# Input projection of block 1 as three rounded products, and the normalise-and-split stages of block 2 shared out over three engines

## The chip, the cores and the metric

One core of a Trainium2 chip runs the whole program in one launch. The time is device microseconds of that core. Five engines run side by side and meet only at semaphores: TensorE (PE in the profile, its weight loads PEld), VectorE (DVE), ScalarE (ACT), GpSimd (POOL) and SyncE (SP, which only issues transfers).
## The reference

Two transformer blocks in float32 on 512 latent tokens and 256 context tokens, 1024 wide. Each begins every sub-layer with a root-mean-square norm and a modulation by a shift and a scale that come from a small matrix product of the condition vector (six of them for each layer). Block 1 has a mixer (attention and gated linear attention) and a mixture of experts; block 2 has two layers of a mixer and a squared-ReLU network.

```python
def modulate(h, shift, scale):
    return h * (1 + scale) + shift
...
    dq_l, dk_l, dv_l, gq_l, gk_l, gv_l, gr_l, lrf_l, lrb_l = split_in_proj(h_lat @ w_in)
    dq_c, dk_c, dv_c, gq_c, gk_c, gv_c, gr_c, lrf_c, lrb_c = split_in_proj(h_ctx @ w_in)
...
def log_gate(lowrank, w2, b):
    return jax.nn.log_sigmoid((lowrank @ w2 + b).astype(jnp.float32)) / GLA_GATE_TAU
```

`w_in` of block 1 is 1024 x 3104: six blocks of 512 columns, and 32 columns at the end, the gate rank (`lrf`, `lrb`, 16 each), which `log_gate` multiplies by a 16 x 256 matrix for each direction.

```python
    for i in range(DEPTH_2):
        ...
        h = modulate_2(rms_norm_2(x, g_norm1[i]), sh1, sc1)
        hc = modulate_2(rms_norm_2(ctx, g_norm1[i]), mc[0], mc[1])
        p = h @ w_in[i]
        ...
        x_new = x_new + gt2 * squared_relu_mlp(modulate_2(rms_norm_2(x_new, g_norm2[i]), sh2, sc2),
                                               ffn_w1[i], ffn_w2[i])
```

## The kernel before

The program is a row of stages. `fence` ends a stage: TensorE, ScalarE, VectorE and GpSimd each drain and wait until all four are there (SyncE only reads the count). Inside a stage each engine runs its own hand-written list; no scheduler reorders it. Tokens lie in six tiles of 128 (`ALLT`: four latent, `LAT`, and two context). PSUM has eight banks of 512 floats.

Four kinds of stage matter here.

- **Normalise, block 1** (`pe_norm`, `act_norm`, `dve_norm`). The scaled tiles `XE` are transposed on TensorE, and ScalarE (first half of the 1024 rows) and VectorE (second half) apply scale and shift while they copy PSUM into `hT`.
- **Input projection, block 1** (`pe_lin`, `each_lin`, `sp_lin` with `BL1`). 32 groups of 8 products of 128 x 128 by 128 x 512, float32, six banks. After each group `pe_mod` does one of 32 modulation steps: 8 products with two columns of condition vectors, four of them side by side on the array, against 2 MB of weights that GpSimd loads into one of two slots (`load_mod`, which waits until the step before the last has run). After every fourth step VectorE copies the sum out (`dve_mod`) and ScalarE writes it to memory and waits for it to land (`act_mod`). Last come six groups of 32 columns for the gate rank.
- **Gates, block 1** (`pe_gates`, `act_gates`, `dve_gates`). The gate rank is transposed tile by tile, copied, multiplied by `w2a`, copied, and goes through Abs, Exp and Ln, each over 3072 columns.
- **Normalise and split, block 2** (`pe_norm_split`, `act_norm_split`, `dve_norm_split`), twice in each of two layers: m = 0 ahead of the input projection, m = 1 ahead of the network (six tiles, but four in m = 1 of the second layer). ScalarE spills x to memory, takes six sums of squares, and for each of the twelve half tiles applies scale and shift into a buffer `NTMP` (four instructions), then rounds it to float32r (`hh`, one instruction). VectorE scales the tiles (`XM`) and subtracts the rounded from the exact one to get the rest (`hl` or `hm`, one instruction for each half tile). For m = 0 the rest lies on top of x, so it waits until the spill has landed. GpSimd meanwhile runs `pool_params2`: it loads seven small parameters, and builds in memory a table `rpbd` of 3840 KB from the position bias, whose landing it waits for before it reaches the fence.

Behind m = 0 comes the projection of block 2 (`pe_proj`), which already is made of three rounded products (`three`: high by high, high by low, low by high). ScalarE rounds each weight piece (`proj_round`), GpSimd makes its rest (`pool_proj`), and GpSimd first issues four loads of the table (`load_table`).

## Time and profile before

| | before |
|---|---|
| median of 3 runs | 4182.31 us (4179.34 to 4189.25) |
| the profiled execution, its time | 4173.02 us |
| its span, first to last instruction | 4171.2 us |
| TensorE busy | 3509.4 us, 84% of the span |
| VectorE, ScalarE, GpSimd busy | 1398.7, 1081.0, 532.9 us |
| mean granted clock of TensorE | 0.916 of 2.4 GHz |

The shares of busy time are means over some forty stages. Since every stage ends in a fence, a stage's length is that of its slowest engine, and what is saved in one stage is saved in the total, unless a transfer that crosses the fence takes it back. A busy microsecond saved on an engine that isn't the last in its stage is worth nothing.

### The profile page before, as it was taken

Reading aid. Unit: us, or ns where it says so; the run is one execution under the profiler, and the core shown is the slowest. Engines: PE = TensorE matmul, PEld = TensorE weight load, DVE = VectorE, ACT = ScalarE, POOL = GpSimd, SP = SyncE. Lnnn points to the kernel's source line nnn. Section 1 sums busy time; section 2 is a strip of 40 time slices with the busy share of each in tenths; the row PEclk is TensorE's granted clock in tenths of the full one; section 3 lists DMA queues with packets and bytes.
Section 4 is the critical chain, followed back from the end, with each engine's and each line's share of the span. In section 5 each row is a group of like instructions: output and inputs, shape, how many; then the busy total and the mean of one; then the engine's idle time right before and its main releaser. Section 6 shows DMA issues by size and latency. Waiting matters only on the chain. (4 is left out here: it accounts for less than half of the span.)

```text
span 4171.2 us, 40026 instructions
## 1 busy us (share of the span) xinstructions
PE 3509.4 (84%) x15659; PEld 2278.5 (55%) x15659; DVE 1398.7 (34%) x2471; ACT 1081.0 (26%) x1967; POOL 532.9 (13%) x427
## 2 busy tenths in 40 slices
PE   5997666587881998788999699999498898997998
PEld 2334554222230784445665388888386455656886
DVE  1104642100003355562112233333364561123444
ACT  2001421111113225443111322121324542104221
POOL 0000000100001425122110000000145222200000
PEclk9997877799995999899999899999799999998999
DMA  7773013699995311002112221221521002223222
GB/s 286 273 274 143 1 44 110 254 428 428 428 428 170 100 37 32 8 1 91 61 61 81 71 71 61 64 68 51 168 77 33 8 34 90 89 81 131 91 91 81
DMA packets 143624, 531.84 MB, mean 128 GB/s; under 512 B 8802, under 2 KB 47128, under 8 KB 120416
## 3 DMA queue, kind: packets, MB, share of 16 engines
q1 hardware_dynamic: 117184, 388.89, 24.8%
q0 software_dynamic: 19792, 102.32, 7.5%
q10 hardware_dynamic: 6480, 38.34, 2.4%
q8 instruction: 112, 1.84, 0.2%
q14 instruction: 56, 0.46, 0.0%
HBM read 486.74 MB, written 42.78 MB: 127 GB/s over the span
## 5 line engine op out<-in xcount | busy, mean ns | idle before, releaser
L507 PE MATMUL ps<-ring,hT 128*128 128x512 f32 (+1 forms) x1056 | 440.1, 576 | 11.8 <-DMA ring<-in_w_out_dram 9.1
L507 PEld LDWEIGHTS ps<-ring,hT 128*128 128x128 f32 x1056 | 196.0, 197 | 255.3 <-issue 252.1
L2556 PE MATMUL ps<-hT_hi,w_hi 128*128 128x512 f32 (+1 forms) x768 | 276.2, 360 | 20.5 <-DVE w_lo L2610 20.5
L1671 PE MATMUL ps<-wp_hi,hT_hi 128*128 128x512 f32 (+2 forms) x608 | 221.8, 365 | 65.6 <-POOL wp_lo L1650 65.6
L2556 PE MATMUL ps<-hT_lo,w_hi 128*128 128x512 f32 (+1 forms) x768 | 276.9, 361 | 0.0
L2556 PE MATMUL ps<-hT_hi,w_lo 128*128 128x512 f32 (+1 forms) x768 | 276.3, 360 | 0.0
L2562 PE MATMUL ps<-w_hi,h_hi 128*128 128x512 f32 x640 | 253.7, 396 | 0.0
L2562 PE MATMUL ps<-w_hi,h_lo 128*128 128x512 f32 x640 | 253.7, 396 | 0.0
L2562 PE MATMUL ps<-w_lo,h_hi 128*128 128x512 f32 x640 | 253.7, 396 | 0.0
L1671 PE MATMUL ps<-wm_hi,hT_hi 128*128 128x512 f32 x480 | 215.6, 449 | 28.4 <-POOL wm_lo L2326 28.4
L1884 PE MATMUL ps<-Z 64*128 64x256 f32 (+3 forms) x576 | 201.7, 547 | 28.3 <-DVE small L2026 12.0
L1673 PE MATMUL ps<-wp_hi,hm_lo 128*128 128x512 f32 (+2 forms) x608 | 220.0, 362 | 0.0
L1672 PE MATMUL ps<-wp_lo,hT_hi 128*128 128x512 f32 (+2 forms) x608 | 219.4, 361 | 0.0
L2356 PE MATMUL ps<-ring,pj 128*128 128x512 f32 x480 | 215.6, 592 | 0.0
L2579 ACT ACTIVATE w_hi<-ring 128x2048 fp32r<-128x2048 f32 x64 | 121.9, 1908 | 328.4 <-PE ps L2562 326.8
L1673 PE MATMUL ps<-wm_hi,hm_lo 128*128 128x512 f32 x480 | 191.8, 400 | 0.0
L1672 PE MATMUL ps<-wm_lo,hT_hi 128*128 128x512 f32 x480 | 191.6, 399 | 0.0
L1443 PE MATMUL ps<-ring,Z 128*64 128x512 f32 x512 | 142.7, 721 | 54.1 <-ACT Z L1465 54.1
L2610 DVE TENSOR_TENSOR w_lo<-ring,w_hi 128x2048 fp32r<-128x2048 f32 x64 | 146.5, 2292 | 80.3 <-ACT w_hi L2579 80.3
L2556 PEld LDWEIGHTS ps<-hT_hi,w_hi 128*128 128x128 f32 x768 | 145.3, 189 | 45.6 <-issue 21.3
L1671 PEld LDWEIGHTS ps<-wp_hi,hT_hi 128*128 128x128 f32 x608 | 115.4, 190 | 84.7 <-issue 66.0
L2632 DVE TENSOR_TENSOR pj<-pj,ps 128x512 f32<-128x512 f32 x140 | 95.5, 686 | 195.0 <-PE ps L2562 195.0
(415 smaller groups left out, 5651.8 us busy)
## 6 DMA issues: line engine op xcount, KB each, us to landing
pj<-in_expert_w_up_dram SPq DMA_DIRECT2D x32, 2048.0 KB, 18.3
pj<-in_expert_w_down_dram SPq DMA_DIRECT2D x32, 2048.0 KB, 19.7
ring<-in_expert_w_gate_dram SPq DMA_DIRECT2D x32, 2048.0 KB, 16.1
ring<-in_ffn_w_dram SPq DMA_DIRECT2D x64, 1024.0 KB, 5.3
Z<-in_w_mod_dram POOLq DMA_DIRECT2D x24, 2048.0 KB, 8.0
ring<-in_w_in_dram SPq DMA_DIRECT2D x46, 1024.0 KB, 5.9
Z<-in_w_ada_dram POOLq DMA_DIRECT2D x8, 2048.0 KB, 8.1
ring<-in_w_in_dram SPq DMA_DIRECT2D x6, 2048.0 KB, 13.0
```

Source lines behind the costliest of these rows:

```text
L507: last = nc.tensor.matmul(bank(i % nb, w), lhs(k, t), s[:, k * w:k * w + w], start=(k == 0), stop=(k == nk - 1))
L1443: last = nc.tensor.matmul(bank(2 + m)[64 * x:64 * x + 64, :], xgT[:, k, 64 * x:64 * x + 64], mslot[2 * m + x][:, 512 * k:512 * k + 512], s ...
L1671: nc.tensor.matmul(out_, a_hi, b_hi, start=first, stop=False)
L1672: nc.tensor.matmul(out_, a_hi, b_lo, start=False, stop=False)
L1673: return nc.tensor.matmul(out_, a_lo, b_hi, start=False, stop=final)
L1884: return nc.tensor.matmul(A.lat(u, x) if k0 == 0 else A.ctx(u, x), S["kq"](p, x, "q")[rs, P * t:P * t + P], S["kq"](p, x, "k")[rs, P * k0: ...
L2356: last = nc.tensor.matmul(bank(6 + u % 2), YB(j % 3, k, t), w[:, 512 * k:512 * k + 512], start=(k == 0), stop=(k == 3))
L2556: last = nc.tensor.matmul(bank(i % 8, c1 - c0), W[a][:, k, :], r[:, k, c0:c1], start=(k == 0 and r is hhk and a == 0), stop=(k == KT - 1 a ...
L2562: last = nc.tensor.matmul(bank(i % 8), H1[hb % 2][a][:, k, P * what:P * what + P], W[b][:, k, :], start=(k == 0 and a == b), stop=(k == 3 ...
L2579: act.activation(WHI[x % 2], raw[x % 4], ACT.Copy).then_inc(w_hi_ok, 1)
L2610: nc.vector.tensor_tensor(WLO[x % 2], raw[x % 4], WHI[x % 2], ALU.subtract).then_inc(w_lo_ok, 1)
L2632: nc.vector.tensor_tensor(y, y, bank(i % 8), ALU.add).then_inc(out_read, 1)
```

## The change

1. Block 1's normalise stage also rounds: ScalarE and VectorE write the modulated half tile to a buffer (`N1T`, in `pj`), then a rounded copy to `hhk`; the twelve rests go to GpSimd (eight, `pool_norm1`) and VectorE (four, `rest1`). They lie on top of x in `xl`, so x is loaded again later (`x_again`).
2. The projection takes the weights in twelve pieces of four row blocks by 512 columns (1 MB) in three slots. ScalarE rounds a piece, VectorE writes its rest over the raw piece, and TensorE does three products for each one before. A group's first four row blocks run in one piece and its last four in the next, so every tile is visited twice; a modulation step follows every second visit, 32 steps as before.
3. The gate rank is computed transposed: weights of 32 columns against 512 and 256 tokens. The gates stage has no transposes; its six products have 33 rows (both directions and a row of ones), Abs reads PSUM, and Exp, Ln and the last VectorE step work in two halves.
4. Block 2's normalise-and-split: ScalarE and VectorE share the sums of squares (half the tiles each) and the half tiles (first half, second half); GpSimd scales every second tile, and makes two of three rests. `NTMP` has a slot for each half tile.
5. `pool_params2` keeps a memset; its transfers are issued by SyncE (`sp_params2`), ahead of the third weight piece. `load_table` moves behind the second piece on GpSimd. The second context is loaded six stages earlier.

```diff
-                    if nb == 6 and i <= 3 * MSTEPS - EARLY:
-                        pe_mod(pe, EARLY + i - 1)
...
-        BL1 = [(0, 512, LAT), (512, 1024, ALLT), (1024, 1536, ALLT), (1536, 2048, ALLT), (2048, 2560, ALLT),
-               (2560, 3072, LAT), (3072, 3104, ALLT)]
+        BL1 = [(0, 512, LAT), (512, 1024, ALLT), (1024, 1536, ALLT), (1536, 2048, ALLT), (2048, 2560, ALLT), (2560, 3072, LAT)]
...
+        def used1(p, x):
+
+            j = x // 2
+            return (w1_half, j + 1) if x % 2 == 0 else (mm_done, p.done(G1[j] + len(BL1[j][2]) - 1))
...
+            for x in range(N1 + 1):
+                if x >= 3:
+                    sp.wait_ge(*used1(p, x - 3))
...
+        def act_split1(act, p, x):
+
+            if x > N1:
+                return
+            act.wait_ge(w1_in[x % 3], 16 * (x // 3 + 1))
+            if x >= 2:
+                act.wait_ge(*used1(p, x - 2))
+            for raw_, hi, _ in w1_parts(x):
+                last = act.activation(hi, raw_, ACT.Copy)
...
+            dve.wait_ge(w1_hi_ok, x + 1)
+            for raw_, hi, lo in w1_parts(x):
+                last = nc.vector.tensor_tensor(lo, raw_, hi, ALU.subtract)
+            last.then_inc(w1_lo_ok, 1)
...
+            for x in range(N1):
+                j, half = x // 2, x % 2
+                pe.wait_ge(w1_lo_ok, x + 1)
+                for m, t in enumerate(BL1[j][2]):
+                    i = G1[j] + m
+                    if half == 0 and i >= 6:
+                        pe.wait_ge(EV[p.own[i - 6]], p.val[i - 6])
+                    for k in range(4 * half, 4 * half + 4):
+                        o = 2048 * (x % 3) + 512 * (k % 4)
+                        last = three(bank(i % 6), hhk[:, k, P * t:P * t + P], hmk[:, k, P * t:P * t + P],
+                                     w1_hi_k(x, k % 4), w1_lo[:, o:o + 512], k == 0, k == KT - 1)
+                    if half:
+                        last.then_inc(mm_done, 1)
+                    elif t == BL1[j][2][-1]:
+                        last.then_inc(w1_half, 1)
+                    q += 1
+                    if q % 2 == 0:
+                        pe_mod(pe, EARLY + q // 2 - 1)
+            pe.wait_ge(w1_lo_ok, N1 + 1)
+            for g, (c0, c1) in enumerate(((0, 512), (512, 768))):
+                i = 32 + g
+                pe.wait_ge(EV[p.own[i - 6]], p.val[i - 6])
+                for k in range(KT):
+                    last = three(bank(i % 6, c1 - c0)[0:32, :], w1_hi[:, 32 * k:32 * k + 32], w1_lo[:, 32 * k:32 * k + 32],
+                                 hhk[:, k, c0:c1], hmk[:, k, c0:c1], k == 0, k == KT - 1)
+                last.then_inc(mm_done, 1)
+
+        def act_lin1(act, n, p):
+            q = 0
...
+                    if half and p.own[i] == "a":
+                        act.wait_ge(mm_done, p.done(i))
+                        act_put(*BL1[j][:2], t, bank(i % 6)).then_inc(evac_a, 1)
+                    q += 1
+                    if q % 8 == 0:
+                        act_mod(act, q // 8)
+                act_split1(act, p, x + 2)
+            act.wait_ge(mm_done, p.done(32))
...
+        def pool_norm1(pool):
+            for i in range(2 * TA):
+                if i % 3 != 2:
+                    rest1(pool, i)
...
+            for t in range(TA):
+                nc.tensor.matmul(bank(t), lrt[t // 4][:, P * (t % 4):P * (t % 4) + P], w2a[0:33, :], start=True, stop=True).then_inc(mm_done, 1)
...
+                act.activation(sp_[:, t, :], bank(t), ACT.Abs)
             act.drain()
-            act.activation(sp_, zc, ACT.Abs)
+            for b in range(2):
...
         def pool_params2(pool, l):
+            pool.memset(rpt, 0.0).then_inc(rp_ok, 1)
+
+        def sp_params2(sp, l):
...
-            pool.wait_ge(rp_in, 32 * l + 16)
-            pool.dma_start(rpbd.ap()[l].rearrange("r (m n) -> r m n", n=P), rpt[0:120, :].unsqueeze(1).broadcast_to([120, 64, P])).then_inc(rp_in, 16)
-            pool.wait_ge(rp_in, 32 * l + 32)
...
+            sp.wait_ge(rp_in, 32 * l + 16)
+            sp.wait_ge(x_out, 16 * (2 * l + 1))
+            sp.dma_start(rpbd.ap()[l].rearrange("r (m n) -> r m n", n=P), rpt[0:120, :].unsqueeze(1).broadcast_to([120, 64, P])).then_inc(rp_in, 16)
...
                 c0, c1 = BL2[l][j][:2]
+                if x == 2:
+                    sp.wait_ge(stage_done, f0)
+                    sp_params2(sp, l)
...
-            load_table(pool, l, 0)
             for x in range(len(R.pieces)):
+                if x == 2:
+                    pool.wait_ge(rp_in, 32 * l + 32)
+                    load_table(pool, l, 0)
...
-                if i >= 3:
-                    act.wait_ge(hl_ok, p.g0 + i - 2)
+            for t in range(nt):
+                act.wait_ge(mm_done, p.done(2 * t))
...
+                act.activation(hhk[:, 0:4, 128 * t:128 * t + 128], NTMP(2 * t).rearrange("p (k n) -> p k n", k=4), ACT.Copy).then_inc(hh_ok, 1)
...
+        def norm_rest(eng, m, g0, i):
+
+            t, h = i // 2, i % 2
+            lo = (hmk, hlk)[m]
+            eng.wait_ge((hh_ok, hh_v)[h], g0 + t + 1)
+            eng.tensor_tensor(lo[:, 4 * h:4 * h + 4, 128 * t:128 * t + 128], NTMP(i).rearrange("p (k n) -> p k n", k=4),
+                              hhk[:, 4 * h:4 * h + 4, 128 * t:128 * t + 128], ALU.subtract)
...
+            V.memset(st[:, 40:41], 0.0)
+            dve.drain()
+            for t in range(na, nt):
+                V.tensor_tensor_reduce(JUNK[1 + t - na], xl[:, t, :], xl[:, t, :], 1.0, st[:, 40:41], ALU.mult, ALU.add, st[:, 16 + t:17 + t])
...
+            scale(0)
+            scale(2)
+            for t in range(nt):
+                if t == 1 and nt > 4:
+                    scale(4)
+                dve.wait_ge(mm_done, p.done(2 * t + 1))
+                for k in range(4):
+                    kk = 4 + k
+                    c = 48 * (t // TL) + 24 * m + kk
+                    last = V.tensor_scalar(NTMP(2 * t + 1)[:, 128 * k:128 * k + 128], bank((2 * t + 1) % 8)[:, 128 * k:128 * k + 128],
+                                           Ac[:, l, t // TL, m, kk:kk + 1], modc[:, l, c:c + 1], ALU.mult, ALU.add)
+                last.then_inc(ht_tmp_v, 1)
+                dve.drain()
+                V.tensor_copy(hhk[:, 4:8, 128 * t:128 * t + 128], NTMP(2 * t + 1).rearrange("p (k n) -> p k n", k=4)).then_inc(hh_v, 1)
             if m == 0:
...
+            pool.wait_ge(rstd_ok, n["rstd"])
+            for t in range(1, nt, 2):
+                pool.tensor_scalar(XM(t), xl[:, t, :], st[:, 32 + t:33 + t], 1.0, ALU.mult, ALU.mult).then_inc(xn_p, 1)
+            if m == 0:
+                pool.drain()
+                pool.wait_ge(x_out, 16 * (2 * l - 1))
+                pool.wait_ge(xn_ok, TA + TL + (p.g0 + nt) // 2)
+            for i in range(2 * nt):
+                if i % 3 != 2:
+                    norm_rest(pool, m, p.g0, i)
 
...
+            sp.wait_ge(stage_done, 4 * 3)
+            sp.dma_start(xl[:, 0:TL, :], I["x"][0].rearrange("(t p) d -> p t d", p=P)).then_inc(x_again, 16)
...
+            sp.dma_start(xl[:, TL:TA, :], I["ctx_2"][0].rearrange("(t p) d -> p t d", p=P)).then_inc(x_in, 16)
```

TensorE at the start of the projection of block 1, before (`ring` holds float32 weights, `hT` the tokens; the rows with `Z` and `small` are a modulation step):

```order
L507 MATMUL ps<-ring,hT 128x512 [waits slot0_in,stage_done]
L507 MATMUL ps<-ring,hT 128x512 x7
L272 MATMUL ps<-Z,small 2x512 [waits mod_slot4_in]
L272 MATMUL ps<-Z,small 2x512 x7
L507 MATMUL ps<-ring,hT 128x512 x8
```

and of the change, from the second product of the eighth row block that it visits, across the first modulation step:

```order
L1838 MATMUL ps<-w_hi,hT_hi 128x512
L1839 MATMUL ps<-w_lo,hT_hi 128x512
L1840 MATMUL ps<-w_hi,hm_lo 128x512
L277 MATMUL ps<-Z,small 2x512 [waits mod_slot4_in]
L277 MATMUL ps<-Z,small 2x512 x7
L1838 MATMUL ps<-w_hi,hT_hi 128x512
```

Eight products between two modulation steps have become 24, and the modulation step itself is the same.

VectorE in the normalise-and-split stage m = 0 of block 2's first layer, before:

```order
L2456 TENSOR_SCALAR small<-small 128x6 [waits sumsq,x_in,stage_done]
L2459 RECIPROCAL small<-small 128x6 [waits std]
L2470 TENSOR_SCALAR pj<-xl,small 128x1024 x6
L2465 TENSOR_TENSOR hm_lo<-Z,hT_hi 128x4x128 [waits hh_ok,x_out]
L2465 TENSOR_TENSOR hm_lo<-Z,hT_hi 128x4x128 [waits hh_ok] x11
```

and of the change (`ISA` is the sum of squares of one tile, three in all; the pair L2651 and L2655 stands six times):

```order
L2629 ISA pj,small<-xl,small 128x1024
...
L2633 TENSOR_SCALAR small<-small 128x6 [waits sumsq]
L2636 RECIPROCAL small<-small 128x6 [waits std]
L2640 TENSOR_SCALAR pj<-xl,small 128x1024 x2
L2651 TENSOR_SCALAR Z<-ps,small 128x128 [waits mm_done]
L2651 TENSOR_SCALAR Z<-ps,small 128x128 x3
L2655 CAST hT_hi<-Z 128x4x128
...
L2618 TENSOR_TENSOR hm_lo<-Z,hT_hi 128x4x128 [waits hh_ok,xn_p,x_out]
L2618 TENSOR_TENSOR hm_lo<-Z,hT_hi 128x4x128 [waits hh_v]
```

VectorE has gained three sums of squares and six half tiles and has lost eight rests, and its four rests now stand behind all its half tiles.

GpSimd at the same place, before:

```order
L1562 DMA Z<-in_gm_w_s_2_dram 128x4x128
L1565 MEMSET Z 128x128
L1567 DMA Z<-in_na_rpb_2_dram 120x31 [waits rp_ok]
L1569 DMA rpbd<-Z 7680x1x128 [waits rp_in]
L1579 DMA Z<-rpbd 64x14x64 [waits rp_in,stage_done]
L1579 DMA Z<-rpbd 64x14x64 x3
```

and of the change (eight rests in six rows, then the first two weight pieces of the projection):

```order
L1719 MEMSET Z 128x128 [waits stage_done]
L2667 TENSOR_SCALAR pj<-xl,small 128x1024 [waits rstd_ok]
L2667 TENSOR_SCALAR pj<-xl,small 128x1024 x2
L2618 TENSOR_TENSOR hm_lo_55<-Z,hT_hi_49 128x4x128 [waits hh_ok,xn_ok,x_out]
L2618 TENSOR_TENSOR hm_lo_55<-Z,hT_hi_49 128x4x128 [waits hh_v] x2
...
L1817 TENSOR_TENSOR wp_lo_57<-ring,wp_hi_56 128x2048 [waits wr_ok,stage_done]
L1817 TENSOR_TENSOR wp_lo_57<-ring,wp_hi_56 128x2048 [waits wr_ok]
L1741 DMA Z<-rpbd 64x14x64 [waits rp_in]
```

The wait for `rp_in`, the table's landing, has moved from ahead of the fence to behind two weight pieces of the next stage.

## Rows read from the trace of the kernel before

**Rows 1.** Timeline, TensorE in block 1's projection: start us, us, engine line op tiles

```profile
72.50 7.13 PE L507 MATMUL ps<-ring,hT 128*128 128x512 f32 x16
...
79.56 1.90 PE L272 MATMUL ps<-Z,small 128*2 128x512 f32 x16
...
81.39 7.13 PE L507 MATMUL ps<-ring,hT 128*128 128x512 f32 x16
```

**Rows 2.** Busy time by stretch: us, PE, PEld, DVE, ACT, POOL, clock, DMA share, GB/s

```profile
100.00:150.00 50.00, 50.00 (x174) 18.87 (x173) 6.20 (x9) 1.79 (x3) 3.80 (x6) 1.00 0.75 281
```

**Rows 3.** Timeline, the six gate-rank groups

```profile
348.22 15.21 PE L507 MATMUL ps<-ring,hT 128*128 128x32 f32 x96
```

**Rows 4.** The chain that ended last, block 2's network: start us, us, what

```profile
3789.07 47.69 PE ps L2556 x192
...
3859.25 22.40 PE ps L2556 x96
```

**Rows 5.** Transfers in block 1's projection: KB each, median us to landing

```profile
Z<-in_w_mod_dram POOLq DMA_DIRECT2D x24, 2048.0 KB, 8.0
```

**Rows 6.** Timeline, block 1's normalise stage and the projection's first product

```profile
53.57 1.37 DVE L472 TENSOR_SCALAR hT<-ps,small 128x128 f32<-128x128 f32 x4 [2.17 <-PE ps L415]
...
62.21 7.13 PE L507 MATMUL ps<-ring,hT 128*128 128x512 f32 x16 [1.87 <-DVEq L214]
```

**Rows 7.** Timeline, the gates stage, up to the next stage's first product

```profile
493.26 1.34 DVE L945 MEMSET hT<- 32x1536 f32 x1 [0.46 <-POOLq L214]
...
505.38 2.76 ACT L937 ACTIVATE Z<-Z 128x3072 f32<-128x3072 f32 x1
...
516.40 3.36 DVE L949 SCALAR_TENSOR_TENSOR Z<-Z 128x3072 f32<-128x3072 f32 x1 [21.80 <-ACT Z L941]
519.84 6.22 PE L964 MATMUL ps<-Z,consts 128*128 128x256 f32 x16 [15.18 <-DVEq L214]
```

**Rows 8.** Timeline, block 2's first normalise-and-split stage and its fence

```profile
1307.93 0.39 SPq L2834 DMA_DIRECT2D xl<-in_ctx_dram  x1
...
1313.27 1.06 ACT L2427 ACTIVATE Z<-xl 128x1024 f32<-128x1024 f32 x1 [10.55 <-DMA xl<-in_ctx_dram]
...
1323.65 1.50 ACT L2441 ACTIVATE Z<-ps,small 128x128 f32<-128x128 f32 x4 [2.33 <-PE ps L2417]
...
1325.77 1.49 ACT L2441 ACTIVATE Z<-ps,small 128x128 f32<-128x128 f32 x4
...
1327.52 2.82 POOL L1569 DMA_DIRECT2D rpbd<-Z  x1 [14.21 <-DMA Z<-in_na_rpb_dram]
...
1328.13 1.29 DVE L2465 TENSOR_TENSOR hm_lo<-Z,hT_hi 128x512 fp32r<-128x512 f32 x2 [2.44 <-DMA xspill<-xl]
...
1349.04 0.69 DVE L2465 TENSOR_TENSOR hm_lo<-Z,hT_hi 128x512 fp32r<-128x512 f32 x1 [1.41 <-ACT hT_hi L2445]
...
1357.00 3.71 ACT L1638 ACTIVATE wp_hi<-ring 128x2048 fp32r<-128x2048 f32 x2 [7.99 <-POOLq L214]
...
1360.40 9.05 POOL L1650 TENSOR_TENSOR wp_lo<-ring,wp_hi 128x2048 fp32r<-128x2048 f32 x2
```

**Rows 9.** Timeline, the same fence in the second layer

```profile
3001.67 3.71 ACT L1638 ACTIVATE wp_hi<-ring 128x2048 fp32r<-128x2048 f32 x2 [7.87 <-POOLq L214]
```

**Rows 10.** Groups of instructions by shape: line engine op, xcount | busy us, mean ns

```profile
L2326 POOL TENSOR_TENSOR wm_lo<-ring,wm_hi 128x2048 fp32r<-128x2048 f32 x24 | 109.3, 4559 | 396.2 <-ACT wm_hi L2317 396.2
L2183 POOL TENSOR_TENSOR Z<-pj 128x256 f32<-128x256 f32 x24 | 14.7, 612 | 52.1 <-ACT pj L2161 51.9
...
L2380 DVE CAST hT_hi<-hT 128x3072 fp32r<-128x3072 f32 x2 | 3.5, 1760 | 17.2 <-DMA hT<-hTd 17.2
...
L2021 DVE CUSTOM_DVE_ANT_0 Z<-ps,Z,small 128x512 f32<-128x512 f32 x5 | 3.8, 751 | 0.6
```

**Rows 11.** Timeline of GpSimd and of VectorE in block 2's first projection

```profile
1402.63 4.79 POOL L1650 TENSOR_TENSOR wp_lo<-ring,wp_hi 128x2048 fp32r<-128x2048 f32 x1 [12.52 <-ACT wp_hi L1638]
...
1403.62 4.36 DVE L835 TENSOR_TENSOR Z<-pj 128x512 f32<-128x512 f32 x1
```

290 lines of the change are left out of this document (182 added, 108 removed).

## Prediction

> **What bounds the kernel now.** I read the page, then the timeline of each stage that the change touches, then groups by shape. No single engine bounds the whole: each stage lasts as long as its slowest engine and the fences add these up. So I cost the change stage by stage, from fence to fence.
>
> In block 1's projection TensorE is never idle. A group of eight float32 products starts at 72.50 and the modulation step behind it at 79.56, the next group at 81.39: 7.06 us and 1.83 us, 8.89 us a period [rows 1]. The granted clock there is 1.00 and the DMA engines are busy 0.75 of the time at 281 GB/s [rows 2]. The six gate-rank groups take 15.21 us for 96 instructions that each produce 32 columns [rows 3]. The rounded form has a price in block 2's network: 96 products of 128 x 512 in 22.40 us, 0.2333 us each, and 47.69 us for the first 192, which is 2.9 us over twice 22.40: the start, which I read as TensorE coming out of idleness on the lower of its clock's two levels [rows 4].
>
> In block 2's normalise-and-split ScalarE sets the pace: four modulations start at 1323.65, the next four at 1325.77, so 2.12 us a half tile and 25.4 us for twelve [rows 8]. VectorE ends at 1349.7, yet the next stage begins at 1357.00 with ScalarE released by GpSimd's queue after 7.99 us: GpSimd had issued the table write only at 1327.52 and waited for its landing [rows 8]. The second layer shows the same, 7.87 us [rows 9]. The first layer also waits for its context: issued at 1307.93, and ScalarE's first square runs at 1313.27 [rows 8].
>
> **The change part by part.** Durations are from the profiled execution.
>
> *Projection of block 1.* Three products for one: 24 x 0.2333 = 5.60 us for the 7.06. I add 0.20 for the passage to the modulation step (an estimate: 16 float32 instructions spaced 0.43 apart end 0.2 short of 7.06). The step stays 1.83. Period 7.63, saving 1.26, times 32: **-40.3**. The start: TensorE now idles longer ahead of the stage, +2.9 [rows 4]; in return the first modulation load (8.0 us [rows 5]) is no longer waited for; before it cost about 1.4 us (first group at 62.21 [rows 6], second at 72.50, one period is 8.89). Together **+1.5**. Gate rank: 24 products over 512 tokens and 24 over 256, 5.6 + 2.8 = 8.4 us, one copy of no more than the 0.69 us that 512 columns take VectorE [rows 8], against 15.2: **-6.2**. Rounding a piece takes 1.9 us on ScalarE (3.71 for two [rows 8]) and its rest about 2.7 on VectorE (four times the 0.69 of 512 columns [rows 8]); a piece lasts TensorE four or six visits, 15 to 23 us, so 4.6 us is hidden, unless ScalarE stands behind a modulation write. Sum -45, between -50 and -38.
>
> The row gives 0.2333 us a product. The Trainium skill, TensorE: Matmul & The Clock Gate, section Back-to-back issue gap, gives about 216 ns for 512 columns on the faster clock; by that the 768 products would be 13 us cheaper. The row is of this very form, so it decides.
>
> *Normalise of block 1.* VectorE was first released at 53.57 and takes 1.37 us for four modulations [rows 6]. Now each of its six half tiles is 1.37, a drain of 0.1 and a cast: 1.760 us for 3072 columns [rows 10] makes 0.35 for 512. That is 10.9 us; a weight rest 2.7, four rests 2.8: 16.4. Meanwhile GpSimd makes eight rests. Its price for 512 columns lies between 0.612 (256) and 4.559 (2048); on the line between them 1.18 [rows 10]. The two engines get in each other's way: a VectorE instruction with two SBUF inputs of 512 columns, 0.69 us elsewhere, took 4.36 us while GpSimd's 4.79 us subtraction ran, and ended with it [rows 11]. A wait is thus bounded by nothing and a whole GpSimd rest, 1.18. I take half, 0.6, on each of six casts, and 1 us over the rests: 21 us, so the projection starts near 75 instead of 62.2: **+12** (+8 without waits, +17 with full ones).
>
> No row shows a cast beside GpSimd. The Trainium skill, SBUF — State Buffer, section Who interferes with whom, says that casts in the two-port mode also take the pair of ports that GpSimd uses, and that the one who comes second is blocked for the whole instruction. By that rule the six waits exist; by the row alone they could be zero and this term +8.
>
> *The stage behind the projection.* Two memsets on VectorE's path (1.34 us for 1536 columns [rows 7], 768 here: 0.7), and 2 MB of x again. At 281/0.75 = 375 GB/s [rows 2] that is 5.6 us of transfer in a stage whose last work is small writes: 0 to 5.6, I take 1.3. **+2**.
>
> *Gates.* Before: 493.26 to 519.84, 26.6 us [rows 7]. After: six products with float32 instructions. TensorE comes from idleness, so near twice the 0.88 us that two instructions take in [rows 1]: 9 us for six (5.3 to 10.5). Then the last Abs 0.6, and from [rows 7] (2.76 for 3072 columns; 505.38 to 516.40 holds three passes and two table loads, so 1.3 a load) 1.3 + 2.8 + 1.3 + 2.8, half of 3.36, and 0.3: 20.1. **-6.5** (-3 to -10).
>
> *Block 2, m = 0, first layer.* The context is there: ScalarE's squares start 4.9 us earlier. Three squares instead of six, each 1.06 us and the read of its sum, about 1.2, save 3.7, but VectorE's three are longer: 0.751 us for 512 columns of an accumulating instruction [rows 10] makes about 1.4 for 1024; net -3.2. Then ScalarE does six half tiles, 12.7 us, and VectorE's six take 10.9 plus one scaling of 0.75; both end near 1328.5. The rests come last: they wait for the spill. It let VectorE go at 1328.13 [rows 8]; issued 4.6 us earlier it should land near 1324. From there GpSimd's eight, VectorE's four and some casts share the port: 9.4 + 2.8 + 1.3, end at 1337.5. The table is no longer waited for at the fence. Next stage at 1338 instead of 1357.0: **-19**. *Second layer*: no context wait to save, but its spill has the queue more to itself: **-16.5**.
>
> *m = 1.* No spill wait, no table. First layer: squares -3.2. Loop 25.4 + 0.8 before; after, VectorE: 6 x (1.82 + 0.6) + 0.75, 1.0 for its later start, rests 4.0: 20.3; together **-9**. Second layer, four tiles: squares -2, 17.8 against 9.7 + 1.0 + 2.0: **-7**. Without port waits each would be 4 to 5 better.
>
> *Start of block 2's projection.* GpSimd began its first rest at 1360.40, 3.4 us after ScalarE, which had that piece ready after 1.9: four table loads stood ahead. Without them -1.5, twice: **-3**. The table (29 us from issue to landing, 1327.52 to about 1356.6 [rows 8]) is now written by SyncE once the spill has landed, at about 1325, and needed by GpSimd behind its second piece, near 1347. It waits there until some 1355, 3 us of loads follow, and TensorE asks for the third piece only after 2 x 18 us of work, near 1378: hidden with 15 us to spare. Queued behind it on SyncE is the third raw piece, needed at about 1360; if it came late it would eat into those 15 us.
>
> **Sum:** -45 + 12 + 2 - 6.5 - 19 - 16.5 - 9 - 7 - 3 = -92. The profiled execution took 4173.0 us: 4081. The median of the runs shown is 9.3 us above it, so **4090** as a median.
>
> **The rivals.**
>
> *Port worse than half* (0.14). Each cast and each VectorE rest waits out a whole GpSimd rest: +5 in block 1, about 5 in each of four stages: 4115. For it: GpSimd's queue of rests is dense. Against: ScalarE delivers only one half tile in 2.1 us, so GpSimd works 1.6 of 2.1.
>
> *No port waits, or cheaper products* (0.13). -4 in block 1, -4 to -5 in the two m = 1 stages, some in m = 0: 4074. A product below 0.2333 us, if weight loads hide better here than in the network, would also end there: each 0.01 is 8 us over 768 products. By the figure of the Trainium skill cited above the estimate would be 4077.
>
> *Transfers bound the projection* (0.06). If each 2 MB modulation load kept the 8.89 us beat, the 40 us are lost: 4130. For it: 0.75 busy would become 0.75 x 8.89 / 7.63 = 0.87. Against: between the step that frees a slot and the one that needs it lie now 7.63 + 5.80 = 13.4 us, and a load takes 8.0 [rows 5].
>
> *The clock falls in the projection* (0.03), the case on the other side. If the dense rounded products alternating with the narrow step were granted the lower level, 1.2 GHz, a period would be 2 x 7.4 + 0.2 = 15 us, 7.4 above forecast. From 92 / 7.4 = 12.4 of 32 periods on, the kernel is slower than before; all 32 make 4325. Against: 1.00 with the same narrow step today [rows 2], and the network's products run at the fast pace [rows 4].
>
> That the change does nothing (0.02, within 0.2%) would need several of these at once.
>
> **How the numbers follow.** The forecast holds 0.62, with its own range 4078 to 4105. To leave out no more than 2 in 10, the range takes in the no-waits case and the bad-port one to about 4114: 4066 to 4114. A measurement of this kernel tells about 0.2% from no change, 8 us. Faster by more than that: all but the clock case and the last, 0.95; same 0.02; slower 0.03.
>
> **What would show it.** In the changed profile: a projection period of 7.6 us and clock 1.0; VectorE's first rests around 70 and the projection's start near 75; the projection stage's end near 331; the gates stage 20 us; the first-layer m = 0 stage 30 us long with `x_out` as the last wait ahead of the rests, no 8 us of GpSimd's queue at the fence; casts of clearly more than 0.35 us where GpSimd is busy. The prediction is wrong if TensorE waits for `w_lo` in the middle of the projection, above all where a modulation write ends a piece and the next is only four visits long, if the third weight piece of block 2 arrives late behind the table, or if the casts wait in full.

## The result and the profile after

The changed kernel takes 4064.16 us (median of four runs, 4061.06 to 4067.18), the kernel before in the same comparison 4180.83: a ratio of 0.9719, 95% interval 0.97 to 0.9738. So the change saves 117 us where I had forecast 92 us, and the time lies 1.8 us below the low end of my range (4066). The direction was right and the size too small by a fifth. The profiled execution took 4065.76 us (span 4063.9), so this time profile and median agree; of the kernel before, the profile I had summed from was 8 us quicker than its median.

In the projection of block 1 the modulation steps are now 7.49 to 7.58 us apart, 7.53 in the mean, instead of 8.89 [rows 1]. Two of them (timeline of TensorE, changed kernel):

```profile
282.81 1.90 PE L277 MATMUL ps<-Z,small 128*2 128x512 f32 x16
290.33 1.90 PE L277 MATMUL ps<-Z,small 128*2 128x512 f32 x16
```

In this stretch TensorE is busy all the time, on the upper level (2.4 GHz, granted clock 1.00), and the busy share of the DMA engines went from 0.75 to 0.88 (busy time by stretch, columns as in [rows 2]):

```profile
100.00:150.00 50.00, 50.00 (x270) 31.02 (x269) 13.45 (x16) 7.75 (x9) 4.78 (x7) 1.00 0.88 335
```

Ahead of it, the normalise stage of block 1 (timeline; its first transposition starts at 49.65 us, where it was 51.49):

```profile
53.18 0.43 DVE L701 CAST hT_hi<-pj 128x512 fp32r<-128x512 f32 x1
...
53.57 2.50 POOL L688 TENSOR_TENSOR hm_lo<-pj,hT_hi 128x512 fp32r<-128x512 f32 x2 [47.65 <-ACT hT_hi L680]
54.98 1.39 DVE L701 CAST hT_hi<-pj 128x512 fp32r<-128x512 f32 x1
...
68.66 2.48 DVE L688 TENSOR_TENSOR hm_lo<-pj,hT_hi 128x512 fp32r<-128x512 f32 x4
71.23 0.79 PE L1838 MATMUL ps<-w_hi,hT_hi 128*128 128x512 f32 x1 [13.39 <-DVEq L219]
```

One cast takes VectorE 0.43 us, the next 1.39: that one lies within GpSimd's two rests (53.57 to 56.07, 1.25 us each). The four rests at the end run at 0.62 us each; GpSimd has finished by then. Behind the projection, the stage that turns the modulations (issue of the last of three small writes, and the next stage's first product):

```profile
345.52 0.31 ACTq L331 DMA_DIRECT2D modd<-Z  x1
...
351.24 1.12 PE L779 MATMUL ps<-consts,pj 128*128 128x128 f32 x4 [25.05 <-ACTq L219]
```

The gates ([rows 7] before): TensorE starts after 12 us of idleness, and its twelve instructions are 0.85 us apart, half the pace of the 0.43 us at which such instructions run on the upper level.

```profile
457.69 10.61 PE L1089 MATMUL ps<-Z,pj 33*128 33x512 f32 x12 [12.03 <-DVEq L219]
```

And block 2's first normalise-and-split, which answers to [rows 8]: the spill is issued and the squares follow at once. GpSimd starts its rests at 1278.41. Its last wait is for VectorE's scaling of a tile, done at 1278.27; the spill has landed just before, 10.8 us after its issue. VectorE makes the last four rests, and ScalarE passes the fence behind VectorE, no longer behind GpSimd's queue.

```profile
1267.40 0.38 ACTq L2594 DMA_DIRECT2D xspill<-xl  x1
...
1267.83 1.06 ACT L2596 ACTIVATE pj<-xl 128x1024 f32<-128x1024 f32 x1 [5.65 <-DVEq L219]
...
1278.41 2.52 POOL L2618 TENSOR_TENSOR hm_lo<-Z,hT_hi 128x512 fp32r<-128x512 f32 x2 [1.68 <-DVE pj L2640]
...
1290.42 2.48 DVE L2618 TENSOR_TENSOR hm_lo<-Z,hT_hi 128x512 fp32r<-128x512 f32 x4
...
1293.33 1.91 ACT L1803 ACTIVATE wp_hi<-ring 128x2048 fp32r<-128x2048 f32 x1 [6.11 <-DVEq L219]
```

I later profiled each kernel twice more. The table sets the lengths of the stages side by side, each from the first instruction behind its fence to the first behind the next. "Change" is the difference of the means of three, "forecast" the term of my sum; the 3 us for the start of block 2's projection stand as 1.5 in each layer.

```
stage                          before (three profiles)    after (three)             change  forecast
start to projection, block 1    62.21   62.06   63.32      71.23   71.52   71.40     +8.9    +12
projection, block 1            301.56  304.70  301.70     252.59  252.47  252.88    -50.0    -45
turn of the modulations         22.41   22.41   22.41      27.42   27.36   27.30     +5.0    +2
attention, block 1             107.08  106.01  107.07     106.45  105.80  105.46     -0.8     0
gates                           26.58   29.92   29.92      21.90   21.90   21.90     -6.9    -6.5
rest of block 1                775.97  776.93  778.76     776.00  776.23  775.72     -1.2     0
normalise, m=0, layer 1         61.19   62.66   59.88      37.74   37.75   37.74    -23.5    -19
projection and attention       998.24  997.65  999.35     995.02  994.19  994.32     -3.9    -1.5
normalise, m=1, layer 1         37.52   37.52   37.56      25.81   25.81   25.81    -11.7    -9
network                        565.35  565.26  565.56     564.65  564.57  564.56     -0.8     0
normalise, m=0, layer 2         43.56   45.37   43.54      24.98   25.47   25.25    -18.9    -16.5
projection and attention       756.29  758.16  755.68     755.84  756.17  755.42     -0.9    -1.5
normalise, m=1, layer 2         26.66   26.66   26.67      19.12   19.11   19.10     -7.6    -7
network and end                386.58  386.09  385.28     385.15  384.45  385.14     -1.1     0
span                          4171.2  4181.4  4176.7     4063.9  4062.8  4062.0    -113.5    -92
```

(The row "normalise, m=0, layer 1" begins 12 us before the stage's fence, with the squares of block 1's end.)

### The profile page after: what moved, and what is told of

Same layout as the page of the kernel before. It is cut to its first block, busy times and chain, and to the rows that moved or that the text cites. A ratio compares the mean times of both kernels' runs of the same rounds, so it can differ in the third digit from the quotient of the medians.

```text
span 4063.9 us, 40443 instructions
## 1 busy us (share of the span) xinstructions
PE 3450.8 (85%) x15843; PEld 2311.0 (57%) x15843; DVE 1472.7 (36%) x2594; ACT 1047.0 (26%) x1853; POOL 585.2 (14%) x459
## 4 chain that ended last, share of the span: by engine, by line
PE 59%; DVE 4%; ACT 2%; DVEq 1%; DMA 1%; issue 1%; POOL 1%; ACTq 0%; POOLq 0%
PE ps L2748 11%; PE ps L2754 11%; PE ps L1838 6%; PE ps L1840 6%; PE ps L1839 6%; PE ps L2523 5%; PE ps L509 4%; PE ps L2051 4%; PE ps L2103 2%; PE ps L2091 2%; PE ps L2085 1%; DVE Z L2651 1%; DVEq L219 1%; DMA ring<-in_w_out_dram 1%; DVE small L2191 0%
## 5 line engine op out<-in xcount | busy, mean ns | idle before, releaser
L509 PE MATMUL ps<-ring,hT 128*128 128x512 f32 x448 | 197.3, 603 | 10.0 <-DMA ring<-in_w_out_dram 9.1
L2493 POOL TENSOR_TENSOR wm_lo<-ring,wm_hi 128x2048 fp32r<-128x2048 f32 x24 | 109.3, 4558 | 394.8 <-ACT wm_hi L2484 394.8
L2748 PEld LDWEIGHTS ps<-hT_lo,w_hi 128*128 128x128 f32 x768 | 145.2, 189 | 24.4
```

The source lines that it names most:

```text
L509: last = nc.tensor.matmul(bank(i % nb, w), lhs(k, t), s[:, k * w:k * w + w], start=(k == 0), stop=(k == nk - 1))
L2493: pool.tensor_tensor(wm_lo[:, 2048 * y:2048 * y + 2048], mring[(3 * j + y) % 4], wm_hi[:, 2048 * y:2048 * y + 2048], ALU.subtract).then_in ...
L2748: last = nc.tensor.matmul(bank(i % 8, c1 - c0), W[a][:, k, :], r[:, k, c0:c1], start=(k == 0 and r is hhk and a == 0), stop=(k == KT - 1 a ...
```

## The experiments

Each `diff` below shows the lines that matter of an edit, cut where `...` stands.

**Which block gives how much, and is the base of the sum to be trusted?** The kernel before again, and the changed kernel with block 2 as before (parts 4 and 5 of the change taken back).

> The kernel before once more, with a second profile. Theory A (the profiled execution of before that the prediction was summed from was a quick one, 7.8 us under the median of its four runs, and the 9.3 us added to the forecast for it are no property of the kernel): the stages that the change leaves alone differ by some us in sum between two profiles of this very kernel, and the offset of profile to median is not 9 us again. Rival B (the stages that the change leaves alone became 5.7 us shorter because of the change): two profiles of the same kernel agree in these stages within 1 us.

> The changed kernel with all of block 2 as before (its normalise-and-split, its parameters and table on GpSimd's queue, its context loaded behind block 1). The trace gives block 1 and its turn a sum of -38 (normalise +10.9, projection -49, stage behind it +5.0, gates -4.7) and block 2's stages -63.5. Theory: -38 to -42 against the kernel before, 4140 or so. Rival: much of block 2's gain comes from elsewhere (a stage that block 1 shortened), then it is below 4125.

```diff
-            pool_norm_split(pool, n, TA, l + 1, 0)
+            plan_split(n, TA)
...
-                    sp_params2(sp, l)
...
+            load_table(pool, l, 0)
```

The kernel before measured 1.0003 of itself (0.9994 to 1.0012). Its second profile is 10.2 us longer than the first: 3.1 in the projection, 3.3 in the gates, 1.5 and 1.8 in the two m = 0 stages, 1.9 in the second layer's attention. The gates show what happens (timeline, first the profile behind my sum, then the second one):

```profile
497.39 7.27 PE L921 MATMUL ps<-Z,hT 17*128 17x256 f32 x24
```

```profile
499.32 10.60 PE L921 MATMUL ps<-Z,hT 17*128 17x256 f32 x24
```

The same 24 instructions, four for each of six tiles. In the first profile four of the six tiles go at the upper level of the clock (0.86 us each) and then it falls; in the second all six go at the lower one (1.71). The gate-rank groups of the projection tell the same: 15.2 us in the first profile, 18.2 in the second, where the granted clock falls at 350.9 us, a few microseconds after they begin. With block 2 as before: 4138.34 us, ratio 0.9898 (0.9882 to 0.9913). Block 1 gives 43 of the 117 us, block 2 the other 74. (The two times of the changed kernel and of this one were not taken side by side, so each share is good to 2 or 3 us; the stage table, from profiles, gives block 2 some 68.) I had forecast 37.5 and 54.5, so block 2 holds most of the miss.

**The context and the spill; the second load of x.**

> The changed kernel with the second block's context loaded where it was before, behind the fence of block 1. Theory (the context's load was in front of the spill, which is why the spill took 15.2 us before and at most 11.0 now): the first square starts 5 us later, the spill is issued 5 us later and lands 15 us after that, the rests of the first layer's stage wait for it, and the stage is 8 us longer (34 instead of 25.5): about +8 us of 4064. Rival: the load costs only its own 5 us and the spill is no later than that: +5, with GpSimd's first rest not waiting for the spill.

```diff
-            sp.wait_ge(stage_done, 4 * 10)
-            sp.dma_start(xl[:, TL:TA, :], I["ctx_2"][0]...)
...
             sp.wait_ge(stage_done, 4 * 16)
+            sp.dma_start(xl[:, TL:TA, :], I["ctx_2"][0]...)
```

4075.16 us; the stage is 43.66 long instead of 37.74, +5.9, between the two expectations. (The profiled execution, 4071.46 us, is the quickest of the five; what makes the median 11 us longer than the changed kernel's and not 6 is not known.) GpSimd now does wait for the spill (timeline of this kernel):

```profile
1285.12 10.55 POOL L2618 TENSOR_TENSOR hm_lo<-Z,hT_hi 128x512 fp32r<-128x512 f32 x8 [4.32 <-DMA xspill<-xl]
```

The context itself is not what the spill shares the DMA engines with: it lands 4.8 us after its issue at 1266.61, and the spill is issued at 1271.53, behind it. What the late context does is to hold the spill back while SyncE's two weight pieces (2 MB), queued behind the context, get going. The DMA traffic between the issue of the spill and its landing shows it, in the kernel before and in the changed one:

```profile
DMA packets 1351, 5.77 MB, mean 380 GB/s; under 512 B 161, under 2 KB 176, under 8 KB 1222
```

```profile
DMA packets 448, 3.77 MB, mean 349 GB/s; under 512 B 16, under 2 KB 16, under 8 KB 320
```

The spill is 3.15 MB of each. Side by side, with other spills:

```
spill of                                  moved until it landed   landed after
before, m=0, layer 1                      5.77 MB                 15.2 us
block2_as_before, the same                5.32 MB                 14.3 us
table_only, the same                      5.47 MB                 14.2 us
context_late, the same                    5.22 MB                 13.5 us
changed, m=1, layer 1                     5.06 MB                 13.8 us
before, m=0, layer 2                      3.71 MB                 10.9 us
changed, m=0, layer 2                     3.81 MB                 11.0 us
changed, m=0, layer 1                     3.77 MB                 10.8 us
```

All that moves, moves at 340 to 386 GB/s, so the landing tells how much else got through meanwhile. That the weight pieces are the cause is read from this table; no kernel here moved them alone.

> The changed kernel with the second load of x (2 MB), and the loads of the output projection behind it on SyncE's queue, issued one fence later, behind the stage that turns the modulations. Theory (the small writes of that stage stand behind 6 MB of loads; their landing rose from 1.5 to 5.2 us): the stage is 3.5 us shorter, 24 instead of 27.4, nothing is late later on, since x and these weights are used six stages on: 4060. Rival: the 4 MB of zeros that GpSimd writes in that stage, which the kernel before wrote too, are what holds the small writes: no change.

```diff
-            sp.wait_ge(stage_done, 4 * 3)
+            sp.wait_ge(stage_done, 4 * 4)
             sp.dma_start(xl[:, 0:TL, :], I["x"][0]...)
```

4061.98 us. The stage is 23.30 us instead of 27.36, as the theory had it (the whole kernel is only 2 us shorter, with no changed kernel timed beside it); 1.6 us after the last small write is issued, the next stage starts, where it was 5.7:

```profile
345.88 0.31 ACTq L331 DMA_DIRECT2D modd<-Z  x1
...
347.49 1.12 PE L779 MATMUL ps<-consts,pj 128*128 128x128 f32 x4 [20.94 <-ACTq L219]
```

GpSimd's zeros, which stay in the stage, do no harm; x and the weights queued behind it do.

**Block 2 in parts, and the port.**

> The changed kernel once more, timed beside the kernels of this call, with a second profile. Theory (the kernel before has run variation in stages that the change replaced: the granted clock falls earlier or later within the gate-rank groups and the gate products, and the table's landing varies; two of its profiles differ by 3.1, 3.3, 1.5 and 1.8 us there): two profiles of the changed kernel agree within 1 us in the same stages, and its times spread less than those of before. Rival: the spread of before is in transfers from memory everywhere; then the changed kernel spreads as much.

Ratio 0.9731 (0.9718 to 0.9745), 4067.43 us. The two profiles agree within 1 us in each stage of the table; the five times spread over 6.2 us, nine of the kernel before, beside them, over 11.0. Over all 14 times of the changed kernel the standard deviation is 2.6 us, over some 70 of the kernel before 4.4. The theory holds, though not all of the spread is gone.

> The changed kernel with block 2's normalise-and-split and its context's load as before, so that of block 2's part only the parameters, the table write and the table loads are moved (to SyncE's queue, and behind GpSimd's second piece). Theory: against the kernel with all of block 2 as before (4138.3) the two fences no longer wait for the table's landing (9.0 and 7.8 us there) and the two projection starts gain 1 us each: -19, 4119. Rival: behind the fence TensorE then waits for a piece that stands behind the table in the queue, and only part of it shows: 4125 or more.

Against block2_as_before only the parameters and the table are as in the changed kernel (part of the diff above, taken back). 4120.09 us, 18.3 below that kernel (4119 expected): the two m = 0 stages are 7.6 and 6.7 us shorter, and the projections behind them 1.4 and 0.6. What the sharing of the stages and the early context give is the rest, 53 us; no run takes the two apart but for context_late, nor the shared squares from the shared half tiles.

> The changed kernel with every rest of the normalised operand on VectorE; GpSimd keeps only its share of the scaling. Theory (VectorE's casts take 1.3 to 1.6 us instead of 0.43 because GpSimd's rest holds the port): all casts 0.43, each six-tile loop 3.2 us shorter, eight more rests at 0.62 each 5.0 us longer: +1.7 in each of four stages, +1 in the short one: +8, 4072. Rival (the long casts wait for something else, such as the modulated data): casts stay long, and the stages are 5 us longer each: +23.

```diff
-            for i in range(2, 2 * nt, 3):
-                norm_rest(dve, m, p.g0, i)
+            for i in range(2 * nt):
+                if i >= 0:
+                    norm_rest(dve, m, p.g0, i)
...
             for i in range(2 * nt):
-                if i % 3 != 2:
+                if i < 0:
                     norm_rest(pool, m, p.g0, i)
```

The same is done to `rest1` in block 1. 4079.14 us against 4067.43 of the changed kernel beside it. All six casts of block 1 take 0.43 us now (instructions of the line of the casts):

```profile
L701 DVE CAST hT_hi<-pj x6: 426/427/429, 53.8 to 65.6; 128x512 fp32r<-128x512 f32 x6
```

So the long casts are GpSimd's doing: shown. The five stages are 1.9, 1.2, 1.6, 1.4 and 0.4 us longer, 6.5 in sum (8 expected). Another 5 us lie in a stage that this kernel doesn't touch, the first layer's projection and attention (999.75 us against 994.2), and 2 us in the two networks. In the attention the granted clock differs; this is one and the same stretch of work, of the changed kernel's third profile and of this kernel:

```profile
1686.00:1862.00 176.00, 140.65 (x705) 80.14 (x702) 94.07 (x208) 78.17 (x164) 40.71 (x50) 0.88 0.12 42
```

```profile
1692.00:1870.00 178.00, 143.57 (x704) 81.80 (x704) 94.12 (x208) 78.17 (x164) 40.03 (x49) 0.85 0.11 42
```

> The changed kernel with GpSimd making ten of twelve rests and VectorE two (seven and one in the four-tile stage). Theory: GpSimd was idle 1.7 us within the loop and ends 2.5 us before VectorE, so two more rests of 1.26 fit, and VectorE's tail of four rests, 2.5 us, becomes one of two, 1.3: -1 us a stage, 4060. Rival: GpSimd becomes the last one, or more casts of VectorE wait for the port: no change or +1 a stage.

```diff
-            for i in range(2, 2 * nt, 3):
-                norm_rest(dve, m, p.g0, i)
+            for i in range(2 * nt):
+                if i % 6 == 5:
+                    norm_rest(dve, m, p.g0, i)
...
             for i in range(2 * nt):
-                if i % 3 != 2:
+                if i % 6 != 5:
                     norm_rest(pool, m, p.g0, i)
```

The same is done to `rest1` in block 1. 4073.24 us, 5.8 slower than the changed kernel: the theory is wrong for block 2. Its stages are 0.1 to 0.7 us longer: the 22 casts take VectorE 26.5 us in sum, 20.9 to 21.3 in the changed kernel, so the port takes back what the shorter tail gives. In block 1 it holds: from the first transposition to the first product 21.0 us instead of 21.6. Both networks are 1.2 us longer as well. In this kernel their first products are spaced 0.43 us for 6.0 and 6.1 us, in the changed one for 3.1 and for 3.1 to 4.0.

**What the clock costs at a start, and between product forms.**

> The changed kernel with two modulation steps behind every four visits of block 1's projection instead of one behind every two. It asks why the rounded products follow one another there in 0.2277 us and in block 2's projection, same instructions, in 0.2325. Theory (the narrow steps in between relieve TensorE, and the relief lasts for the next products): over 48 products in a row the spacing rises toward 0.2325 in the second half of each run. Rival (it is the layout of the operands): 0.2277 in all 48. The loads of the modulations have less slack: two steps of 1.83 in a row and then 11 us; a wait for a load of up to 1 to 3 us a pair shows how near the projection is to being bound by transfers.

```diff
-                    if q % 2 == 0:
+                    if q % 4 == 0:
+                        pe_mod(pe, EARLY + q // 2 - 2)
                         pe_mod(pe, EARLY + q // 2 - 1)
```

This kernel was timed once, at 4062.07 us. Both expectations on the spacing fall: within a run of 48 products some stretches have 0.227 us, others alternate between 0.224 and 0.236, and the spacing doesn't rise toward the end. Why block 1's products come every 0.2292 us in the mean (0.2276 to 0.2313 from one run of 24 to the next), those of block 2's projection every 0.232 and those of the network every 0.234 stays open. But the stage is 247.61 us instead of 252.65, and TensorE waits 0.35 us in all for modulations: 32 of 64 changes between the product forms are gone, and 5.0 us with them, some 0.15 us each. In the changed kernel's trace the first product behind a step is followed only 0.336 us later.

> The changed kernel with idle TensorE kept busy ahead of four stage starts of block 2: products of 128 x 512 into a bank that nobody reads, 22 (8 in the four-tile stage) behind the last transposition of each normalise-and-split and 24 or 12 behind the fence; they change nothing that is computed. Theory (every stage that TensorE enters from idleness begins on the lower level of its clock: the first products there are spaced 0.43 instead of 0.23 for 4.7, 3.1, 5.2 and 3.9 us in the four starts of the changed kernel, 3.0 to 6.0 in others, and this is where most of the difference between two executions, and the rest of the gain, lies): the four starts go at the fast pace, half of 16.9 us is saved: -8, 4057. Rival (the level at a start depends on something else, or falls again in the wait for the first piece): no change, or the stages are longer because the extra products are late: +2.

```diff
+            pe.wait_ge(ht_tmp, p.g0 + 4)
+            pe.wait_ge(hh_ok, p.g0 + 4)
+            keep_busy(22 if nt > 4 else 8)
+
+        def keep_busy(count):
+            for _ in range(count):
+                nc.tensor.matmul(bank(4), hhk[:, 0, 0:P], hhk[:, 0, 0:512], start=True, stop=True)
...
             fence(pe, n)
+            keep_busy(24)
             pe_proj(pe, n, l)
...
             fence(pe, n)
+            keep_busy(12)
             pe_ffn(pe, n, l)
```

4064.7 us, the same as the changed kernel beside it (4064.82). The extra products ahead of the first network (timeline of TensorE) are fast before the fence (22 in 5.27 us), and 3.90 us of idleness later the other twelve start slow (4.61 us):

```profile
2311.79 5.27 PE L2597 MATMUL ps<-hT_hi 128*128 128x512 f32 x22 [1.70 <-ACT hT_hi L2617]
2320.97 4.61 PE L2597 MATMUL ps<-hT_hi 128*128 128x512 f32 x12 [3.90 <-DVEq L219]
```

They take the slow stretch on themselves: the real products start at 2325.41, as soon after the fence as ever, 0.23 us apart. The two networks are 1.3 and 1.5 us shorter, the second layer's projection and attention 4.7. In the first layer the projection is 1.9 us shorter, but the attention behind it 6.7 us longer (791.3 us; 784.4 to 784.9 in the three profiles of the changed kernel). It spends 78 us on the lower level of the clock there, against 68 to 72, and gives the gain back.

> The kernel of the line above with the second load of x and the output projection's weights one fence later as well. Theory: both savings add, -3.7 beside the -8: 4053. Rival: they don't, since what is saved in the stage behind block 1's projection is waited for later.

4057.39 us, 4053 expected. The first layer's projection and attention take 995.46 us and not 999.27, though nothing in them differs from the kernel above; the later load of x gives its 4.0 us.

> The changed kernel a third time, timed beside the two kernels above. Theory: its stage starts on the lower clock level last 3 to 5 us again, the same within about 1.5 us per start as in its other profiles, and the total is 4064 to 4067.

4064.82 us; the four starts are slow for 3.9, 3.1, 5.1 and 4.0 us, as in the theory.

> The kernel before a third time, with a third profile. Theory: the first profile was quick in places where the granted clock happened to stay high (the gate-rank groups, 1.00 for longer; four of six gate products at the fast pace) and where the table landed early; a third profile lies like the second in most of them: projection with gate rank 303 to 305 us against 301.5, gates 28 to 30 against 26.6, the two table stages 1 to 2 us longer each. Rival: the second was the odd one, and the third repeats the first.

4179.38 us. The theory is right for the gates alone: 29.92 us, as in the second profile. The projection (301.70) and the second table stage (43.54) repeat the first profile, and the first table stage (59.87) is 1.3 us below it. So of the three the first was quick in the gates alone; the rest of the 10 us is spread over places that differ from one execution to the next.

> The changed kernel with six float32 products of 128 x 512 into a bank that nobody reads, issued ahead of the fence in front of the gates, while TensorE would wait 12 us for the norm on VectorE. Theory (the six gate products go at 1.71 us each because TensorE enters from idleness, on the lower level; the first profile of before shows four of them at 0.86): some of the six go at 0.86 and the stage is up to 4 us shorter: 4062. Rival: the clock stays low all the same, since the stage before keeps TensorE too little busy: no change.

```diff
             pe_attn(pe, n, *da_spec())
+            pe.wait_ge(evac_a, n["a"])
+            pe.wait_ge(evac_v, n["v"])
+            for _ in range(6):
+                nc.tensor.matmul(bank(7), ident, C(0, 512), start=True, stop=True)
             fence(pe, n)
```

4066.76 us: no change, the gates are 21.89 us again. Six float32 products go at the fast pace before the fence (12 instructions in 5.32 us); after 6.88 us of idleness the gate products are on the lower level all the same:

```profile
445.65 5.32 PE L3100 MATMUL ps<-consts 128*128 128x512 f32 x12
457.84 2.92 PE L1089 MATMUL ps<-Z,pj 33*128 33x512 f32 x3 [6.88 <-DVEq L219]
```

> Modulation steps in pairs, and the second load of x one fence later, in one kernel. Theory (each change from rounded products to a float32 step and back costs about 0.4 us, the pairs halve their number and saved 4.9 us of the projection in the one look; the later load saved 3.7): -8.5 against the changed kernel, 4056 to 4058. Rival: the pair's gain was the clock's or the loads' luck: -4.

4057.03 us (4053.88 to 4063.57): projection 247.98, turn 23.39. Both gains are there.

> The pairs, the later load, and TensorE kept busy ahead of the four starts of block 2 and ahead of the gates. Theory: -8.5 and about 3 more from the starts and up to 4 from the gates: 4050 to 4054. Rival: stages of attention that nobody touched fall to a lower mean clock, as they did in one of the two kernels that kept TensorE busy, and give the 4 us back.

4052.57 us (4051.58 to 4054.89), ratio to the kernel before 0.9693 (0.9679 to 0.9706): a version faster than both kernels, 12 us below the changed one. Its pieces: later x -4.1, pairs -2.5 (the projection is 250.10; one modulation is waited for 1.68 us), the two networks and the second layer's projection and attention -7.4, given back by 0.9 in the first layer's; the gates gain nothing.

## Why the prediction was right in kind and too small

The stages that I named gave the gain, but terms of the sum were mis-sized, and no one of them alone makes the 25.8 us. The largest misses are the projection (50.0 gained for 45), the first layer's m = 0 stage (23.5 for 19), the base (4), block 1's normalise stage (8.9 lost for 12), and the first m = 1 stage (11.7 for 9). Against these stands the turn of the modulations, which lost 5 for 2. One step was wrong in kind, not only in size: that the first layer's rests of m = 0 wait for the spill.

**The base.** I took 4173.0 for the profiled execution of before and added 9.3 us to come to a median. The mean of three profiles is 4178.3, so 4 us of the 25.8 I was off are this step: I treated the offset as a constant that the changed kernel would keep. Part of it was a lucky clock in the gates, a stage that the change replaces.

**Projection, -45.** Measured -50, of which 1.1 is that the second profile of before was slow in its gate-rank groups; against the first it is -49.0. The period is 7.53, not 7.63, since the products are spaced 0.2292 in the mean, not 0.2333: 0.1 times 32 is 3.3 us of the miss, and this price is the step that failed. (The 0.216 us that the prediction quotes beside it was reached nowhere in this stage: the shortest spacing is 0.224.) The start cost what I had put down: the first step comes 8.25 us behind the first product, where a group on the upper level takes 5.7, so 2.6 for the slow first products, less the 1.4 of before, makes +1.2 for +1.5. (The first modulation load is still waited for, 0.4, 0.9 and 0 us in the three profiles, where I had said it would not be.) The gate rank went from 15.55 us to 9.05, -6.5 for -6.2. Rounding and rests of the weights are hidden, as I had said: TensorE waits for nothing else in the stage. Transfers don't bind (0.88 busy, 0.87 forecast by the rival).

**Normalise of block 1, +12.** From the first transposition to the first product 10.7 us became 21.6: +10.9. The port waits I had assumed at 0.6 on each of six casts are 0.8 to 1.1 on four of them, 3.9 us against 3.6; but the last four rests take 2.5 us, where I had 3.8. The other 2 us I had no term for: the stage starts earlier, at 49.6 to 50.6 us in every kernel here with the new projection, at 51.3 to 52.6 in the three profiles of before. Ahead of it ScalarE writes four small rows to memory and reads them back once they have landed: 2.3 us from the first write to the read (44.32, 46.60), where it was 5.1 (42.98, 48.12). Before, 4 MB of projection weights stood in SyncE's queue at that point, now 3 MB; that this is the reason is likely and not tested. The rule of the Trainium skill, SBUF — State Buffer, section Who interferes with whom, that a cast in the two-port mode is held up by GpSimd, agrees with this: 1.26 to 1.53 us beside GpSimd, 0.43 with GpSimd's rests taken away.

**Turn, +2.** Measured +5. I named the 2 MB of x and took 1.3 of a bound of 5.6. The failed step is that choice: the three small writes that end the stage landed 5.2 us after their issue where it was 1.5, beside x and the weights queued behind it. Taken away, they give back 4.1 us; the 0.9 that stays is near the 0.7 I had for the memsets.

**Gates, -6.5.** -4.7 against the first profile, -6.9 against the mean. The six products take 10.6 us (9 forecast, upper bound 10.5), all of them on the lower level. (My terms for this stage add up to 19.8 us, not 20.1.)

**Block 2, m = 0: -19 and -16.5.** Measured -23.5 and -18.9. In the first layer the step that failed is "The rests come last: they wait for the spill". I had it land near 1324, 16 us behind the fence, because I carried over the 15.2 us of before, and then charged the rests of both engines one after the other, 13.5 us. It lands 10.8 us after it is issued, no later than the last scaling that GpSimd's rests wait for, and eight rests are made under the loop. The 15.2 us were those of a spill held back by the context until 2 MB of weights and GpSimd's parameters were under way; the trace of before had the other case as well, the second layer's spill, which landed in 10.9. With the context brought back it takes 13.5 us and GpSimd waits 4.3. In the second layer GpSimd waits 1.8 us for the spill, and the stage is as short (25.0 to 25.5 us behind its fence). The table step held: 18.3 us measured for what I had put at two fence waits of 7.9 and 3 us of earlier starts, of which the projections behind the two stages show 1.5 and 1.1.

**m = 1: -9 and -7.** -11.7 and -7.6. I charged 4.0 us for the last rests, with port waits; GpSimd is done by then and they take 2.5. So 1.5 of the 2.7 us is the same port charged twice, once on the casts and once on the tail. Of the other 1.2, the squares give 0.4 (3.6 us saved for 3.2) and VectorE's loop 0.6 (14.7 us from its first modulation to its first rest, for 15.3).

**Stages that nothing touches.** -3.9 in attention, networks and the rest of block 1, and 2.4 more than forecast in the first layer's attention. In the rest of block 1 the -1.2 is noise: the stage has 774.5 to 778.8 us over all the kernels here. The slow stretch at the start of the first layer's network is 3.1 us in all three profiles of the changed kernel and 4.8 to 5.6 in those of before; half of the difference is gained. In the second layer's network it is 3.1 to 4.0 against 3.4 to 6.0. That the lower level is the reason is shown by the kernels that kept TensorE busy; what decides how long it lasts isn't, nor where the 2.4 us come from.

Of the rivals, a worse port, transfers that bind and a falling clock in the projection did not occur. "No port waits, or cheaper products" (4074) named a true part, the products; the port waits were there.

## What to carry to other kernels

When a term is priced by a stage that will be replaced, look at how that stage varies between executions: an offset between profile and median lives somewhere, and the change may remove the place. Ask of each transfer that a stage waits for what else will move until it has landed: 3 MB took 15.2 us while 2.6 MB of other transfers got through, and 10.8 while 0.6 MB did, and a 1.5 us write became 5.2 beside bulk loads. A duration read in one place need not hold once the order of the queue has changed; look for a second place in the same trace. A resource that two engines share is to be charged where both are busy, not again where one is done.

## What the runs showed of the hardware

TensorE lost the upper clock level in short pauses: products at the fast pace, 3.90 us idle, then products at half pace (kept_busy); the same after 6.88 us (gates_kept_busy). At the four starts of block 2 where nothing kept it busy, it ran at half pace for 3.0 to 6.1 us, which costs half of that, and in the first layer's network kernels that differ in no more than who makes two rests differ there by 3 us (3.1 and 6.0). A 512-column rest takes GpSimd 1.25 us and VectorE 0.62 in a row (0.69 alone); a 512-column cast takes VectorE 0.43 alone and up to 1.57 beside GpSimd. A change between float32 and rounded products costs TensorE some 0.15 us (mod_pairs, pairs_x_late). A 3 MB spill landed in 10.8 to 15.2 us with 3.7 to 5.8 MB moved in all meanwhile, at 340 to 386 GB/s.
